# The first layer of a hybrid diffusion trunk on one core: filter generation moved ahead of the first norm, modulation blocks set singly between the projections

## What is computed

```python
m = (silu(cond) @ w_mod[l] + b_mod[l]).reshape(6, D_MODEL)   # for c_ctx and for c
h = modulate(rms_norm(x, norm1_g[l]), m[0], m[1])            # x * (1 + scale) + shift
p = h @ w_in                                                 # q, ff, fb, v, g, hy0..hy2
o_a = hgrn2 scans of q, ff, fb, v (both directions), head norm, * silu(g)
filt = sin(fr2 * (sin(fr1 * (z @ w1 + b1)) @ w2 + b2)) @ w3 * window     # constant positions z
z = vh * x1                                                  # of the short convolution of hy
o_b = (fft_conv(z, filt[:, 0]) + flip(fft_conv(flip(z), filt[:, 1])) + hbias * z) * x0
x = x + m[2] * (concat(o_a, o_b) @ w_out)
x = x + m[5] * hier_moe(modulate(rms_norm(x, norm2_g[l]), m[3], m[4]))
```

## Time and profile before

| what | value |
|---|---|
| runs | median 1201.1 us of 3 (1198.02 to 1202.69) |
| the profiled execution | 1203.07 us, its span 1201.2 us |
| granted TensorE clock, mean over the span | 0.974 |
| PE busy | 1107.4 us, 92% of the span |
| chain that ended last | PE 79%, DMA 13%, DVE 4%, ACT 2%, issue 1% |
| bytes moved by DMA | 326.21 MB, mean 272 GB/s |

### The profile page before, as it was taken

The page is one execution under the profiler, slowest core; times in us unless marked ns, Lnnn a source line. Parts: engine busy times, 40 slices in busy tenths (PEclk is TensorE's granted clock), DMA queues, the critical chain, the costliest instruction groups (busy, mean ns, idle before and its releaser), DMA issues.

```text
span 1201.2 us, 13459 instructions
## 1 busy us (share of the span) xinstructions
PE 1107.4 (92%) x5106; PEld 533.0 (44%) x5106; DVE 388.7 (32%) x982; ACT 237.5 (20%) x522; POOL 94.4 (8%) x160
## 2 busy tenths in 40 slices
PE   4998899999999999988999989999899899889998
PEld 1444455455546543333333344455655433333334
DVE  3331225244344531111111165463745311111113
ACT  3221110324232400000000142243544000000001
POOL 0000020101100001001010110000000011000110
PEclk9798999999999999999999999999999889999999
DMA  9854483424373957999959862322019999999964
GB/s 386 338 210 201 187 309 144 155 98 194 124 307 125 427 219 324 426 427 427 394 240 407 350 237 79 115 80 83 22 69 426 373 412 427 427 415 424 425 274 155
DMA packets 32982, 326.21 MB, mean 272 GB/s; under 512 B 6141, under 2 KB 7549, under 8 KB 15008
## 3 DMA queue, kind: packets, MB, share of 16 engines
q1 hardware_dynamic: 22032, 295.94, 59.9%
q0 software_dynamic: 10896, 29.52, 6.6%
HBM read 312.97 MB, written 22.28 MB: 279 GB/s over the span
## 4 chain that ended last, share of the span: by engine, by line
PE 79%; DMA 13%; DVE 4%; ACT 2%; issue 1%; DVEq 0%; SPq 0%; POOLq 0%; ACTq 0%
PE bank L1889 20%; PE bank L1811 14%; PE bank L1905 11%; PE bank L1803 9%; DMA arena<-in_moe 8%; PE bank L2097 7%; DMA ring<-in_proj 2%; PE bank L2019 2%; PE bank L1722 2%; DMA h_rows<-hT 2%; PE bank L1847 1%; PE bank L2064 1%; PE bank L1952 1%; PE bank L2081 1%; PE bank L1915 1%
## 5 line engine op out<-in xcount | busy, mean ns | idle before, releaser
L1889 PE MATMUL bank<-arena,cT 128*64 128x512 f32 x880 | 239.1, 597 | 4.6 <-DMA arena<-in_moe 3.0
L1811 PE MATMUL bank<-ring,hT 128*128 128x512 f32 x384 | 169.8, 597 | 3.0 <-ACT hT L786 3.0
L1889 PE MATMUL bank<-ring,cT 128*64 128x512 f32 x464 | 150.3, 609 | 9.1 <-DMA ring<-in_moe 5.7
L1889 PEld LDWEIGHTS bank<-arena,cT 128*64 128x64 f32 x880 | 77.5, 138 | 123.3 <-issue 123.3
L1905 PE MATMUL bank<-arena,hT 128*64 128x512 f32 x512 | 116.3, 608 | 12.9 <-ACT hT L866 8.9
L1803 PE MATMUL bank<-hT,ring 128*128 128x384 f32 x320 | 112.6, 513 | 8.9 <-DMA ring<-in_proj 7.1
L1811 PEld LDWEIGHTS bank<-ring,hT 128*128 128x128 f32 x384 | 72.1, 191 | 88.7 <-issue 87.1
L1471 DVE TENSOR_TENSOR hT<-bank,hT 128x512 f32<-128x512 f32 x21 | 14.5, 692 | 289.1 <-PE bank L1889 289.1
L1803 PEld LDWEIGHTS bank<-hT,ring 128*128 128x128 f32 x320 | 63.5, 201 | 54.7 <-issue 9.9
L2097 PE MATMUL bank<-cT,ring 128*128 128x384 f32 x256 | 86.1, 492 | 0.0
L1889 PEld LDWEIGHTS bank<-ring,cT 128*64 128x64 f32 x464 | 48.2, 140 | 82.4 <-issue 82.4
(11 more groups left out here) (311 smaller groups left out, 1116.2 us busy)
## 6 DMA issues: line engine op xcount, KB each, us to landing
arena<-in_moe SPq DMA_DIRECT2D x66, 2048.0 KB, 20.8
ring<-in_proj SPq DMA_DIRECT2D x41, 2048.0 KB, 8.9
ring<-in_moe SPq DMA_DIRECT2D x30, 2048.0 KB, 18.6
y_rows<-cT POOLq DMA_DIRECT2D x12, 512.0 KB, 8.0
arena<-y_rows POOLq DMA_DIRECT2D x12, 512.0 KB, 6.5
h_rows<-hT POOLq DMA_DIRECT2D x6, 512.0 KB, 16.9
arena<-in_hyconst SPq DMA_DIRECT2D x1, 2432.0 KB, 18.5
xT<-in_x SPq DMA_DIRECT2D x1, 1536.0 KB, 6.3
```

Source lines behind the costliest of these rows:

```text
L1811: ins = mm(ps[:, :], src[:, k, P * i : P * i + P], w[:, k, :], start=k == 0, stop=k == KD - 1)
L1889: ins = mm(psum[kind][rows, :], mo["hS"][:, k, rows], w[side].rearrange("p (k n) -> p k n", k=KD)[:, k, :], start=k == 0, stop=k == KD - 1)
```

## The change

The list of steps is written anew. The filters' steps go to the front, with the squares of x (square1), their sum on DVE (add1) and the rest of the norm (sum1) between them; G is cut into two halves, one behind the first modulation turn, one behind apply1. Behind that each modulation block stands alone: hy0, block 4, hy1, block 5, hy2, block 6, q and so on, where before two stood together after each projection. Eleven blocks come ahead of the scans where thirteen did, so the weave of the scans has two more. On SP the positions, the filters' weights, the windows and the forward transforms are issued ahead of the blocks, the first two also ahead of x; the inverse transforms alone stay behind the fifth block, with a semaphore of their own. No arithmetic is added or removed.

```diff
 STEPS0 = [
-    ("sum1",), *MODS[0:3], ("hf1",), MODS[3], ("apply1",),
-    *project("hy0")[:1], ("hf2",), *project("hy0")[1:], ("hf3",), *MODS[4:6], ("G",),
-    *project("hy1"), *MODS[6:8],
-    *project("hy2"), *MODS[8:10],
-    *project("q"), ("zt",), ("even", "v", 0), ("dft",), ("even", "v", 1), ("even", "v", 2), *MODS[10:11], ("inv",),
-    *project("ff"), *MODS[11:13],
-    *scans_with(project("fb") + MODS[13:15] + project("g") + MODS[15:20] + out_half(0, 1)[:5]),
+    ("hf1",), ("square1",), ("hf2",), ("add1",), ("hf3",), ("sum1",), *MODS[0:2], ("G", 0), *MODS[2:4], ("apply1",), ("G", 1),
+    *project("hy0"), MODS[4], *project("hy1"), MODS[5], *project("hy2"), MODS[6], *project("q"), ("zt",),
+    ("even", "v", 0), MODS[7], ("dft",), ("even", "v", 1), ("even", "v", 2), MODS[8], ("inv",), MODS[9],
+    *project("ff"), MODS[10],
+    *scans_with(project("fb") + MODS[11:14] + project("g") + MODS[14:20] + out_half(0, 1)[:5]),
...
+FILTER_HALVES = [range(0, 4), range(4, len(FILTER_DFT))]
...
             sp.dma_start(con[:, 0:first_consts], consts_d[:, 0:first_consts]).then_inc(consts_in, 16)
+            sp.dma_start(hy["hyc"][:, 0:T], hyconst_d[:, 0:T]).then_inc(filter_in, 16)
+            sp.dma_start(hy["hyp"], hypar_d).then_inc(filter_in, 16)
             sp.dma_start(xT[:, :, :], x_d).then_inc(x_in, 16)
+            sp.dma_start(hy["hyc"][:, T:inverse], hyconst_d[:, T:inverse]).then_inc(hyconst_in, 16)
...
-                    if n == MOD_FIRST - 2:
-                        sp.dma_start(hy["hyc"][:, 0:T], hyconst_d[:, 0:T]).then_inc(filter_in, 16)
-                        sp.dma_start(hy["hyp"], hypar_d).then_inc(filter_in, 16)
...
-                        sp.dma_start(hy["hyc"][:, T:], hyconst_d[:, T:]).then_inc(hyconst_in, 16)
+                        sp.dma_start(hy["hyc"][:, inverse:], hyconst_d[:, inverse:]).then_inc(inverse_in, 16)
...
-            def norm_sums(layer):
-                act.preload_act_table_set("natural_log_exp_and_others")
+            def norm_squares(layer):
...
+            def norm_factor(layer):
...
+                elif kind == "square1":
+                    act.wait_ge(x_in, 16)
+                    norm_squares(0)
                 elif kind == "sum1":
-                    norm_sums(0)
+                    act.preload_act_table_set("natural_log_exp_and_others")
+                    norm_factor(0)
...
-                elif kind == "sum1":
+                elif kind == "add1":
                     for k in range(1, KD - 1):
                         add_square(0, k, hT[:, 0, :])
+                elif kind == "sum1":
                     norm(0)
...
-                    for g, (seq, part, m) in enumerate(FILTER_DFT):
+                    for g in FILTER_HALVES[half]:
+                        seq, part, m = FILTER_DFT[g]
...
                 else:
+                    pe.wait_ge(inverse_in, 16)
                     pe.wait_ge(spec_ready, 3)
```

More of the change, by code:

```diff
@@ L267, in groups_of @@
         return [("ot", u)] if layer == 0 else []
+    if kind == "G":
+        return [("G", g) for g in FILTER_HALVES[u]]
     return {
-        "sum1": [("norm1", 0)], "hf3": [("hf3", i, half) for i in range(NT) for half in range(2)], "apply1": [],
-        "G": [("G", g) for g in range(len(FILTER_DFT))], "zt": [("zt", i) for i in range(NT)],
+        "sum1": [("norm1", 0)], "square1": [], "add1": [], "hf3": [("hf3", i, half) for i in range(NT) for half in range(2)], "apply1": [],
+        "zt": [("zt", i) for i in range(NT)],
         "dft": [(g, s) for s in range(len(SIGNAL_DFT)) for g in ("Ur", "Ui")], "inv": [("inv", ch) for ch in range(4)],
@@ L389, in trunk_kernel @@
         first_params, first_consts = PARAMS.at["lower"][0], CONSTS.at["eps"][0] + 1
-        filter_in, hyconst_in = sem("filter_in"), sem("hyconst_in")
+        filter_in, hyconst_in, inverse_in = sem("filter_in"), sem("hyconst_in"), sem("inverse_in")
+        inverse = HYCONST.at["inv_lat"][0]
         s0_in, caches_in = sem("s0_in"), sem("caches_in")
@@ L969, in _ @@
             nc.scalar.activation(condT[:, :, 0:2], pr("cond").rearrange("p (k s) -> p k s", s=2), ACT.Silu).then_inc(cond_ready, 1)
-            act.wait_ge(x_in, 16)
             act.wait_ge(consts_in, 16)
@@ L986, in _ @@
                 elif kind == "G":
-                    for g in range(len(FILTER_DFT)):
+                    for g in FILTER_HALVES[u]:
                         full(act, "G", g)
@@ L1030, in _ @@
             experts(0)
-            norm_sums(1)
+            act.preload_act_table_set("natural_log_exp_and_others")
+            norm_squares(1)
+            norm_factor(1)
             norm_shift(1)
@@ L1925, in experts, with hyena @@
                     ins.then_inc(full_of("yt", layer, k), 1)
-            def hyena(kind):
+            def hyena(kind, half):
                 if kind == "hf1":
@@ L2135, in _ @@
                     ins.then_inc(full_of("ot", u), 1)
-                elif kind not in ("apply1", "square_heads", "shift_logits"):
-                    hyena(kind)
+                elif kind not in ("apply1", "square1", "add1", "square_heads", "shift_logits"):
+                    hyena(kind, u)
             norm2(0)
```

## The result

The changed kernel takes 1182.55 us, the median of 4 runs (1178.44 to 1184.05), against 1200.59 of 4 runs before (1198.02 to 1202.69): a ratio of 0.984, interval 0.9824 to 0.9857. It is 18.0 us faster where 29.6 were forecast. The profiled execution took 1183.99, its span 1182.1, at a mean granted clock of 0.980; 19.1 less than that of before, so a reading of the two traces has 1.1 more gain to share out than the medians. The sign holds and the time lies in the range, but two fifths of the gain are missing.

A forecast was written before the change was run, and what follows sets the result against it. PE's own work was taken as the bound, 79% of the chain, with 13% transfer waits. 1203.07 - 12.3 - 11.9 - 5.6 + 0.2 = 1173.5 profiled, so 1171.5 against 1201.1; range 1163 to 1186, chance 0.81.

The forecast's parts named there:

- The start: Filters moved ahead of hy0: hy0 begins 9.0 later, 21.35 behind its start goes, so the start gains 12.3 us.
- I take 7.8: Time of hf3 in the new start, taken between 5.34 at the high clock and 10.7 at the low.
- the text's 46.0: Forecast start of hy0 in us, at the end of the new start's chain; 9.0 later than before.
- Rival 1: Filters' chain keeps PE at low clock to hy0, which starts at 70: 1199, halfway 1186; chance 0.07.
- The single blocks: One modulation block between projections: both ring waits behind hy1 and hy2 and their low clock go, 11.9 us gained.
- ff: Projection whose load waits behind block 9's: 12.5 of loads against some 12.8 of work, costed at nothing, bound 2.
- The weave: Two more blocks among the scans: outputs of second and fourth units wait less for DVE, 5.6 us gained, bounds 0 and 7.6.
- What was costed at nothing: POOL's clearing some 30 us earlier, inverse matrices landing by 43, no expert load asked for before the mixer's end: no cost.
- Rivals 2 and 3: Rival 2: layer 0's experts' weight waits absorb the gain, 1201, chance 0.05. Rival 3: new order makes loads late, 1211, 0.04.
- A granted clock near 0.5 between 20 and 45: Sign that the forecast was wrong: the profile's clock column low in the start, at 20 to 45 us.
- hy0 beyond 52: Sign that the forecast was wrong: first projection tile beginning later than 52 us, where near 46 was forecast.
- the signs for being right: hy0 near 46, no ring load in the chain at 50 to 200, scans some 24 earlier, mixer's end some 30 earlier.

The follow-up runs named there:

- the constants' kernel: The changed kernel with 4, 7 and 7 matmuls of constants, results never read, ahead of hf1, hf2 and hf3: 1174.34 us, ratio 0.9769.
- the single blocks alone: The kernel before, its own start and load order kept, with only modulation blocks set singly and the new weave: 1189.52 us, ratio 0.9909.
- zero rows: The changed kernel with hf1, hf2 and hf3 over all 128 rows of PE, the rows added holding zeros: 1175.05 us, ratio 0.9782.
- the single blocks with G behind hy1: The kernel before with modulation blocks set singly and the new weave, and G moved to behind hy1: 1186.18 us, ratio 0.9858.
- constants over 64 rows: The changed kernel with four matmuls of constants, filling 64 of 128 rows, ahead of each of hf1, hf2 and hf3: 1178.89 us, one run.
- block 0 early: The changed kernel with matmuls of constants ahead of hf1 and hf2, and the first modulation block loaded and computed ahead of hf3: 1181.7 us, ratio 0.9822.

## Why the prediction came out as it did

**The start was mis-sized, at "I take 7.8" for hf3 and at full rate for all behind it.** The mechanism was right: the filters moved into time in which PE stood still, and hy0's first tile came back to 5.16. The size was not. The forecast had hy0 at 46.0 (its own terms add up to 45.8), the trace has 52.79, 6.8 more. They lie so: hf3 begins at 17.35 in place of 16.0 (1.35; in_hypar lands at 6.62, and hf1 and hf2 take 1.5 each); hf3 takes 10.61 in place of 7.8 (2.8); the norm 2.86 in place of 1.3 (1.55); the two blocks and the turn behind them 1.3 more. From G to hy0 16.6 passed, as the terms add up; the text's 46.0 left 16.8 for it. So some 5.6 of the 6.8 are half rate, and the constants' kernel gives all of it and more back: hy0 at 44.08.

My 7.8 came from the tiles behind the ring waits, which lose 2 to 3 us at first. Those tiles fill 128 rows; hf3 fills 64. With 128 rows and the same rests hf3 took 8.15, so the estimate was good for the matmul that it was read from and not for the one that it was used on. The bounds of the text (hy0 at 43.5 to about 70) had the truth between them; the choice near the first was the error.

The Trainium skill (TensorE: Matmul & The Clock Gate, section HAM oscillation) says that short bursts behind waits start at the halved clock each time; the prediction worked out 2.9 more by it and set it aside. In the changed kernel hf3 came out as by that rule, 2.8 more than I took. But the runs don't leave it at that. With the same rests and full rows hf3 took 8.15, and with no rest and half rows it took 10.61. So waits alone do not give the time of hf3 here; the rows filled, or the share of the array, count as well, and of that the section says nothing.

Rival 1 (a start at low clock up to hy0, 1186 to 1199) is in part what happened: the low rate lasted through the norm and into the blocks, to about 33 us (an estimate: the blocks' 4.79 are 1.2 above 3.57, so the first 2.4 of them were at half rate), not to hy0. What the prediction held against it, that PE has work without a gap from hf3 on, did not protect the start: the first 16 us of that work ran at half rate.

**The single blocks were right, and are most of the gain.** Both ring waits and both slow tiles are gone. The two terms after them were costed near nothing, and came to 1.6 together: ff, which I had at nothing with 2 as a bound, waits 0.80 for a load of 13.38 (12.5 forecast) and its first tile takes 0.26 more than the 6.87 of its others, at a granted clock of 1.00; the decays at the scans' opening wait 0.78, where 0.2 were allowed. What the prediction missed is that the gain has a second side: without the single blocks the new start makes a third ring wait of 5.05, and would have been worth nothing.

**The weave was right**, 6.2 against 5.6: the waits of 2.71 and 1.83 are gone, and the wait at L2147 is 0.6 shorter. With the two blocks put back the kernel loses 9.9, of which 5.0 are the ring wait of three blocks in a row.

**What was costed at nothing, was nothing.** No wait for the inverse transforms or for DVE's windows shows in the chain; DVE, paced by the slow hf3, has its last window at 30.07, ahead of G at 36.19. Two readings of that part were off without harm: POOL's clearing starts 24.0 earlier (132.82 against 156.84), not some 30, and six experts' loads are asked for ahead of the output projection's last half and not behind it, from 380.65 before and from 358.69 now.

**Rivals 2 and 3 fell.** The experts' waits start 20.8 and 22.6 earlier and are 0.1 shorter and 1.7 longer; behind the second the kernel is still 20.9 ahead. So the gain passes through the experts, and the loads move with PE as the earlier trace rows had it. Behind the mixer 2.9 of 22.0 are given back, 1.1 ahead of the first of these waits and 1.8 behind the second. From the mixer's end on the kernel before takes 819.1, the single blocks alone 818.6, zero rows 820.3, the constants 821.9 and the single blocks with G behind hy1 822.2, so this part scatters by some 3.5 and doesn't follow the length of the gain. The two traces show where the 2.9 lie: in PE's rate behind rests that both kernels have. L1838 (L1849 in the changed kernel) stands ahead of the experts' first wait; the 48 matmul instructions of L1811 (L1822) open layer 1's projections; before, then in the changed kernel:

```profile
417.95 7.18 PE bank L1838 x48
...
710.20 22.54 PE bank L1811 x48
```

```profile
395.99 8.41 PE bank L1849 x48
...
690.18 23.45 PE bank L1822 x48
```

That is 1.2 and 0.9 more, with the granted clock over these stretches at 0.65 where it was 0.77, and 0.89 where it was 0.93; another 0.9 lies in layer 1's first norm, ahead of the second group (2.47 where it was 1.54). The first group takes 5.60 in the single blocks alone and with zero rows, and 8.50 with the constants, so its rate differs from kernel to kernel at a place that none of them touches. Why it does is open.

**The range held in part by luck.** Its upper end allowed 6 for the start, 2 for ff and 5.6 for the weave. The start and the second stage missed 6.8 and 1.6, and the 2.9 behind the mixer had no allowance; the measured time is inside because the weave did not need its own.

**Of the signs that the prediction named**, one failed as a sign. "A granted clock near 0.5 between 20 and 45" was to show a slow start. The windows of the changed kernel (length, busy PE, PEld, DVE, ACT, POOL, granted clock, DMA share, GB/s) read so:

```profile
10.00:20.00 10.00, 4.19 (x5) 1.45 (x6) 7.27 (x15) 5.63 (x11) 0.00 (x0) 1.00 1.01 429
20.00:30.00 10.00, 10.00 (x14) 3.85 (x12) 8.02 (x13) 0.00 (x0) 0.00 (x0) 1.00 0.85 364
```

The column says 1.00, while hf3's matmuls take 10.61 / 5.41 = 1.96 times as long as at full rate: by their length they run at the 1.2 GHz level, not at 2.4. In the kernel with block 0 early the same 10.61 stand under a column of 0.50. The other sign, hy0 beyond 52, was the one that told. Of the signs for being right, the scans begin 20.4 earlier in place of 24 and the mixer ends 22.0 earlier in place of 30, and one ring load is in the chain between 50 and 200, ff's at 176.22, though PE waits only 0.80 for it.

The earlier trace rows at 10 to 20 has the same column of 1.00 in the kernel before, and the norm's first sum there takes 1.62, against 0.91 in the constants' kernel:

```profile
14.02 1.62 PE L1738 MATMUL bank<-hT,con 128*128 128x384 f32 x2 [14.02 <-DVE hT L1108]
```

Had I compared lengths in place of that column, I would have had the low rate at the start in the kernel before.

## What to carry to other kernels

Between two projections that stream their weights through a ring, put one small block and not two, and look at every place where several blocks follow each other: the wait moves to whichever place has the shortest cover, as two kernels here show at hy1 and ahead of the scans. Look also at what a block that goes had covered itself: G waited 3.19 for its filters where one block was left. Work that is moved into time in which PE stands still is not done at the rate that the same rows have elsewhere: cost it by the lengths of matmuls of the same shape behind the same rests, and where the shape fills few rows, add rows of zeros (1175.05) or matmuls of constants ahead of it (1174.34 against 1182.55). A single wait of 2.75 us ahead of such work undid that again, so the cover must hold up to it.

## What was not expected of the hardware

- While matmuls that fill 64 of 128 rows ran from a start at half rate, PE stayed at it, even without rests: hf3 10.61 in three kernels (the changed one, constants over 64 rows, block 0 early), 8.15 with zero rows added, 5.41 behind constants over 128 rows. At full rate once, they stayed there (0.85, 0.86, 5.41, with rests of 0.60 and 0.50 between); behind a rest of 2.75 they did not.
- The granted clock of the profile reads 1.00 at the start of the execution while matmuls take nearly twice their length (10.61 against 5.41 at 17 to 28 us); in the kernel with block 0 early, behind a stretch at full rate, it reads 0.50 for the same length. The Trainium skill (TensorE: Matmul & The Clock Gate, section Seeing it yourself) warns that clock events of a trn2 trace have been seen to be unreliable; this agrees.
